# The scores' second product on 64 rows of TensorE instead of 128

## What is computed

```
def block_attention(q, k, v, bias_fn, scale):
...
        sc = jnp.einsum('bhqd,bhkd->bhqk', qb, k).astype(jnp.float32) * scale
        p = jax.nn.softmax(sc + bias_fn(qi, ki), axis=-1).astype(v.dtype)
...
def attn_mixer(h_lat, h_ctx, w_in, q_g, k_g, sink, w_out, need_ctx):
...
    s_loc = jnp.einsum('bnqkgd,bnskd->bnkgqs', qb, kb).astype(F32)
...
    s_ctx = jnp.einsum('bnqkgd,bckd->bnkgqc', qb, kc).astype(F32)
```

## Time and profile before

| | us |
|---|---|
| median of 3 runs | 2715.04 (2712.72 to 2723.18) |
| profiled execution, its own time | 2712.89 |
| its span from first to last instruction | 2711.2 |
| TensorE matmul busy in it | 2561.4 (94%) |
| VectorE busy | 1160.6 (43%) |
| ScalarE busy | 1021.3 (38%) |
| GpSimd busy | 979.1 (36%) |

### The profile page before, as it was taken

How to read it: one execution, slowest core, us unless ns; L and a number is a source line. 1 busy time by engine, 2 the same in 40 slices (tenths; PEclk the granted TensorE clock), 3 DMA queues, 4 the chain that set the end, 5 groups by cost and what they waited for, 6 DMA issues and landing times.

```text
span 2711.2 us, 34706 instructions
## 1 busy us (share of the span) xinstructions
PE 2561.4 (94%) x13544; PEld 2137.2 (79%) x13544; DVE 1160.6 (43%) x2127; ACT 1021.3 (38%) x1862; POOL 979.1 (36%) x519
## 2 busy tenths in 40 slices
PE   5998999999999999999999999999999999898898
PEld 4986788888788678888878878888888888787666
DVE  3356599520336659941151222421122242456564
ACT  4455344432445444443332322212232222345542
POOL 3322356765432235676532212322221233321121
PEclk9999999999999999999999999999999999999999
DMA  4211244322321225433221011111101111110000
GB/s 157 71 51 63 86 171 171 100 94 94 108 68 39 71 88 200 148 101 109 92 70 48 15 32 39 63 63 55 48 16 32 40 63 63 58 58 29 28 28 32
DMA packets 54018, 200.63 MB, mean 74 GB/s; under 512 B 5984, under 2 KB 5984, under 8 KB 52960
## 3 DMA queue, kind: packets, MB, share of 16 engines
q1 hardware_dynamic: 51696, 188.65, 20.9%
q10 hardware_dynamic: 2160, 9.76, 1.0%
HBM read 196.29 MB, written 2.10 MB: 73 GB/s over the span
## 4 chain that ended last, share of the span: by engine, by line
PE 73%; DVE 15%; ACT 4%; POOL 4%; issue 3%; DMA 0%; DVEq 0%; ACTq 0%; POOLq 0%
PE ps L529 40%; PE ps L549 16%; DVE arena L1791 7%; PE ps L579 7%; PE ps L889 5%; POOL wl L2329 2%; DVE arena L1980 1%; PE ps L736 1%; DVE arena L1977 1%; POOL norm_acc L2342 1%; ACT wh L1140 1%; PE ps L1100 1%; DVE norm_sq L1754 1%; PE ps L752 1%; PE ps L1085 0%
## 5 line engine op out<-in xcount | busy, mean ns | idle before, releaser
L2329 POOL TENSOR_TENSOR wl<-wring,wh 128x1024 fp32r<-128x1024 f32 (+1 forms) x305 | 765.4, 2510 | 1337.5 <-ACT wh L1140 1324.7
L1140 ACT ACTIVATE wh<-wring 128x1024 fp32r<-128x1024 f32 (+1 forms) x305 | 317.0, 1042 | 678.9 <-PE ps L529 650.3
L529 PE MATMUL ps<-hh,wh 128*128 128x512 f32 x1104 | 431.9, 391 | 9.3 <-DVE hl L1766 7.3
L529 PE MATMUL ps<-hl,wh 128*128 128x512 f32 x1104 | 430.7, 390 | 0.0
L529 PE MATMUL ps<-hh,wl 128*128 128x512 f32 x1104 | 430.7, 390 | 0.0
L529 PEld LDWEIGHTS ps<-hh,wh 128*128 128x128 f32 x1104 | 207.8, 188 | 55.8 <-issue 7.0
L529 PEld LDWEIGHTS ps<-hh,wl 128*128 128x128 f32 x1104 | 207.9, 188 | 43.7
L529 PEld LDWEIGHTS ps<-hl,wh 128*128 128x128 f32 x1104 | 207.9, 188 | 40.8
L549 PE MATMUL ps<-hh,wh 128*128 128x512 f32 (+1 forms) x504 | 215.1, 427 | 5.6 <-DVE hl L2310 3.0
L549 PE MATMUL ps<-hh,wl 128*128 128x512 f32 (+1 forms) x504 | 203.2, 403 | 0.0
L549 PE MATMUL ps<-hl,wh 128*128 128x512 f32 (+1 forms) x504 | 202.0, 401 | 0.0
(11 more groups left out here) (292 smaller groups left out, 5131.7 us busy)
## 6 DMA issues: line engine op xcount, KB each, us to landing
wring<-wts SPq DMA_DIRECT2D x290, 512.0 KB, 3.4
arena<-wts SPq DMA_DIRECT2D x48, 512.0 KB, 4.3
wring<-wts SPq DMA_DIRECT2D x16, 384.0 KB, 3.0
xL<-xt SPq DMA_DIRECT2D x1, 2048.0 KB, 9.3
arena<-tab SPq DMA_DIRECT2D x1, 2048.0 KB, 16.5
arena<-cv ACTq DMA_DIRECT2D x2, 1024.0 KB, 4.7
arena<-tab ACTq DMA_DIRECT2D x1, 2048.0 KB, 7.9
out_t<-xL ACTq DMA_DIRECT2D x8, 256.0 KB, 2.0
```

Of the source, the lines that this page charges most:

```text
L529: mm = nc.tensor.matmul(o[0], a, b, start=start and k == first and j == 0, stop=stop and k == last and j == 2)
L1140: nc.scalar.activation(wh[:, sn % SPLIT_SLOTS, :kn * w], raw(u)[:, :kn * w], ACT.Copy).then_inc(act_done, tick("act", ("hi", u)))
L2329: G.tensor_tensor(wl[:, sn % SPLIT_SLOTS, :kn * w], raw(u)[:, :kn * w], wh[:, sn % SPLIT_SLOTS, :kn * w].bitcast(F32), ALU.subtract).then_inc(
```

## The change

The keys' low parts are written to one half of the partitions only (in the layers that half in which the head's high queries stand, in the last stage the lower half), so one VectorE instruction falls away for each. The second product takes the 64 rows of that half: queries' high parts by keys' low parts. The product of low parts by low parts is no longer computed. In the last stage all high queries go to partitions 0 to 63 and all low queries to 64 to 127, where before the halves alternated with the head. In the built program the second products have a tile of 64 rows (in 48 of them at row 64), and the first products keep one of 128.

```diff
-                            a = qs_sets[n % 2][:, h % 2 if kind == "fox" else c, qs]
-                            bs = [t[n % 2][:, h % 2 if kind == "fox" else c, 0:ke] for t in (kh_sets, kl_sets)]
+                            x = h % 2 if kind == "fox" else c
+                            r = slice(64 * x, 64 * x + 64)
+                            pairs = [(qs_sets[n % 2][:, x, qs], kh_sets[n % 2][:, x, 0:ke]),
+                                     (qs_sets[n % 2][r, x, qs], kl_sets[n % 2][r, x, 0:ke])]
...
                         nc.tensor.matmul(dst, q, akh[:, g % 2, first:first + w], start=True, stop=False)
-                        last = nc.tensor.matmul(dst, q, akl[:, g % 2, first:first + w], start=False, stop=True)
+                        last = nc.tensor.matmul(dst, q[0:64], akl[0:64, g % 2, first:first + w], start=False, stop=True)
...
-                    nc.scalar.activation(aqs_t[r, g % 2, :, q, 128 * t:128 * t + 128],
+                    nc.scalar.activation(aqs_t[0:64, g % 2, :, q, 128 * t:128 * t + 128],
...
-                            for d in (slice(0, 64), slice(64, 128)):
-                                V.tensor_tensor(kl_sets[n % 2][d, i, :], ps[r, b, :],
-                                                kh_sets[n % 2][d, i, :].bitcast(F32), ALU.subtract).then_inc(
-                                    dve_done, tick("dve", *([("kl", l, n)] if i and d.start else [])))
+                            V.tensor_tensor(kl_sets[n % 2][r, i, :], ps[r, b, :],
+                                            kh_sets[n % 2][r, i, :].bitcast(F32), ALU.subtract).then_inc(
+                                dve_done, tick("dve", *([("kl", l, n)] if i else [])))
...
-                for r in (slice(0, 64), slice(64, 128)):
-                    V.tensor_tensor(akl[r, g % 2, o:o + w], ps[r0:r0 + 64, b, 0:w], akh[r, g % 2, o:o + w].bitcast(F32),
-                                    ALU.subtract).then_inc(
-                        dve_done, tick("dve", *([("ktl", g, part)] if r.start else [])))
+                V.tensor_tensor(akl[0:64, g % 2, o:o + w], ps[r0:r0 + 64, b, 0:w],
+                                akh[0:64, g % 2, o:o + w].bitcast(F32), ALU.subtract).then_inc(
+                    dve_done, tick("dve", ("ktl", g, part)))
...
-                for q, (r, other) in enumerate(((slice(0, 64), slice(64, 128)), (slice(64, 128), slice(0, 64)))):
-                    V.tensor_tensor(aqs_t[other, g % 2, :, q, c], ps[r, b, 0:256].rearrange("p (x b) -> p x b", x=2),
-                                    aqs_t[r, g % 2, :, q, c].bitcast(F32), ALU.subtract).then_inc(
+                for q, r in enumerate((slice(0, 64), slice(64, 128))):
+                    V.tensor_tensor(aqs_t[64:128, g % 2, :, q, c], ps[r, b, 0:256].rearrange("p (x b) -> p x b", x=2),
+                                    aqs_t[0:64, g % 2, :, q, c].bitcast(F32), ALU.subtract).then_inc(
```

More of the change, by code:

```diff
@@ L732, in _ @@
                                 pe.wait_ge(pool_done, at("pool", "mk0", l))
-                            a, bs = mq[0:96, h, qs], [mk[h][0:96, 0:ke]]
+                            pairs = [(mq[0:96, h, qs], mk[h][0:96, 0:ke])]
                         claim([s % 3], "dve", "sm", l, s)
-                        for x, b in enumerate(bs):
+                        for x, (a, b) in enumerate(pairs):
                             last = nc.tensor.matmul(ps[:, s % 3, 0:ke], a, b, start=x == 0,
-                                                    stop=x == len(bs) - 1 and kind != "fox")
+                                                    stop=x == len(pairs) - 1 and kind != "fox")
                         if kind == "fox":
```

## The result

The kernel with the change takes 2769.7 us (median of 4 runs, 2764.8 to 2772.2), the kernel before 2717.0 us in runs beside it: a ratio of 1.0185, interval 1.0173 to 1.0197, or +52.8 us. The forecast was 2779 us within 2742 to 2812, so direction and mechanism hold.

The account below looks back on a forecast made before the run. TensorE was taken to bound the kernel, busy for 2561.4 of 2711.2 us. From 2712.9 us, 87 for tile changes, less 10 and 13 hidden and 3 for VectorE, plus 5 for the clock, gave +66: 2779 us, range 2742 to 2812.

Parts of the forecast that it names:

- mechanism: Layers' and last stage's scores: 448 changes between 128-row and 64-row tiles each empty TensorE, 87 us before hiding.
- the two signs: At score pairs, the second product's weight load starts with its own matmul, and that product 0.32 us behind a 512-column first.
- the second product costs nothing: Rival for the scores: 64-row weights are brought forward as before, only VectorE's saving is left; 2710 us, chance 0.08.
- 64 rows save time on TensorE: On the second products the prediction claimed the opposite: 64 rows in place of 128 save nothing on TensorE.
- The price: Each change of tile around the second products costs TensorE 0.195 us; 448 of them make 87 us.
- The half price: Rival for the tile changes: only the load or only the emptying is exposed, +27, 2740 us; chance 0.10.
- What is hidden: TensorE's existing waits absorb part of the 87 us: 10 us in the layers, 13 us in the last stage.
- a group of 16 units has one wait of up to 2.7 us for ScalarE's copy, behind about two units: Last stage: this wait hides 1.6 us per group, part of the 13 us taken as hidden there.
- VectorE's 3 us: Dropped low-key instructions free 21 us of VectorE, but save only 3 us, at the layers' `diff` ends.
- The clock's 5 us: Mainly last stage: dearer tile changes at 1.2 GHz, 2 us, and one or two more clock falls, 3 us; bounds 0 and 20.
- the third rival: Last stage: sparser TensorE work makes the clock fall in each group of units; +96, 2809 us, chance 0.12.

Follow-up runs that it names:

- The 96 rows: Low keys in one half, zeros in the other; second product takes rows 0 to 95 in the last stage and half the layers' scores: 2708.8 us, 0.9967 of the kernel before.
- the zeros: The change, but zeros in the low keys' other half and the second product over all 128 rows: 2710.4 us, 0.9973 of the kernel before; repeats 2707.4 and 2709.2 us.
- the grouped order: The change, but in the last stage a score's two first products come ahead of its two second ones: 2753.8 us, 1.0124 of the kernel before.
- the kernel with zeros in the layers alone: Low keys in one half, zeros in the other, 128-row second products, in the layers only; last stage as before: 2717.2 us, 0.9997 of the kernel before.

## Why the prediction came out as it did

**The mechanism was right.** A change of tile costs TensorE time wherever it does not wait anyway, and the two signs that the prediction named are there: the load starts with its own matmul, and the second product starts 0.33 us behind a first one of 512 columns. The 96 rows, the zeros and the grouped order leave the change of tile as the only account of those tested. That the second product costs nothing, and that 64 rows save time on TensorE, are both out.

**The price was right within 5%.** Both kernels have the same 13544 matmuls in the same order, so the distances between their starts can be subtracted one by one. At the full clock and without waits the medians are +0.093 us into the 64-row product, +0.19 behind it (out, with the exposed load of the one before), and for the matmul after that +0.10 where it is a product (a mask matmul or another of 128 columns), as forecast, but only +0.057 where it is a transposition. Per score that is 0.39 or 0.34 us in the layers, 0.37 on average, and 0.78 or 0.74 in the last stage, mostly 0.74 (0.39 and 0.78 in the prediction). 96 x 0.37 + 64 x 0.74 = 83 us, against 87. The 4 us are the 81 scores with a transposition behind them. The half price was wrong: load and emptying are both paid, as the 36-row matmuls had shown.

**What is hidden: right in the layers, too small in the last stage.** In the layers 96 x 0.37 = 36 us stand against 21 to 24 measured at the same clock: 12 to 15 us hidden, where the prediction had 10 and up to 3 of VectorE. In the last stage 64 x 0.74 = 47 us stand against 28.9 in the profiled pair and 28 to 30 at the same clock: 18 us hidden where it had 13. This is the step "a group of 16 units has one wait of up to 2.7 us for ScalarE's copy, behind about two units": there are six waits for that copy in the stage. At the seventeen second products behind which TensorE had to wait, the idle time went from 19.8 to 7.6 us. By the windows, the time without a matmul in flight fell from 27.5 to 13.9 us. The other 4 to 5 us may be changes that stand next to a wait, where the emptying falls into time in which TensorE had nothing to do. That last part is argued, not shown.

**VectorE's 3 us** are inside what the runs allow (0 to 5 us in the change, about 1 us in the kernel with zeros in the layers alone).

**The clock's 5 us did not come.** In the profiled pair it seemed to: the time at 1.2 GHz went from 82 to 107 us. But 13.6 us of that lie in the mLSTM part, which the change doesn't touch and where this time varies between executions of one kernel too (three traces of the zeros kernel have 24, 27 and 41 us from the end of the layers' scores to the last stage). In the last stage, where the prediction expected the lower stretches to grow, they went from 27.3 to 23.9 us. Over all executions both kernels average 0.982. So the term should have been zero, and the third rival, the clock giving way in each group of units, did not come.

The sum with what was measured is 83 - 13 - 18 = 52 us, where the same-clock columns give 50 to 52; the 13 and the 18 are themselves differences to those columns, so this is bookkeeping and no second proof. The forecast of +66 was 14 us above it: 4 from the price, 5 from the clock, and 5 from what is hidden in the last stage. All three errors went the same way. In the absolute time 4 us of them were offset by luck, since the profiled execution from which the forecast started had the highest clock of the 53 whose clock is known.

## What to carry to other kernels

Before cutting a matmul's contraction from 128 to 64 rows, look at its neighbours: between 128-row matmuls every entry and every exit cost 0.17 to 0.20 us here, more than the 256-column product itself (0.12). Zeros in the unused rows keep the tile, cost a few short memsets on GpSimd (0.52 us each in the layers, 1.4 us in the last stage) and give the benefit of the work that was dropped elsewhere; where 64 rows can't be avoided, put such products side by side. When two kernels differ by less than half a per cent, compare executions at the same granted clock before explaining anything, since one kernel's runs scattered by 8 us along it; then ask whether the clocks themselves differ, since that is part of what the kernel does.

## What was not expected of the hardware

A product of 96 rows costs what 128 rows cost (1.27 us for the same score, 2708.8 against 2710.4 us in all), so that what matters is on which side of a step between 64 and 96 rows it stands. A transposition after an exit pays only 0.057 us more, where a product of 128 columns there pays 0.10, as the 256-column one after the 36-row matmuls did. The mean granted clock of the kernel before varied from execution to execution between 0.980 and 0.985, and that of the zeros kernel between 0.981 and 0.986, and the falls come also in stretches whose code did not change. The same last-stage code stood at 1.2 GHz for 27 us in one trace and for 44 in another.
